# Block 0's MLP in seven half-size products per pair, with part of the weight splitting on GpSimd

## The reference

```
n = rmsnorm(x);  [pool in 512 | q 512 | k 128 | v 128 | pool gate 1024 | attn gate 1024] = n @ w_in
pool = (trailing means over 2/4/8/16 frames - frame) @ w_pool * pool_scale
attn = banded attention of q, k, v (8 query heads, 2 kv heads, rotary, sinks, window 2 chunks of 64)
h = x + (sigmoid(gp) * pool + sigmoid(ga) * (attn @ w_attn_up)) @ w_out
h = h + relu(rmsnorm(h) @ w_up)^2 @ w_down        # w_up 1024 x 4096, w_down 4096 x 1024
y = rmsnorm(h)
```

## Time and profile before

| | |
|---|---|
| median of 3 runs | 2354.0 us (2353.39 to 2355.53) |
| span of the profiled execution | 2351.3 us |
| instructions | 41109 |
| PE busy | 2325.9 us |
| DVE busy | 1642.2 us |
| ACT busy | 1075.6 us |
| GpSimd (POOL) busy | 350.2 us |

### The profile page before, as it was taken

The page is one execution under the profiler, slowest core; times in us unless marked ns, Lnnn a source line. Parts: engine busy times, 40 slices in busy tenths (PEclk is TensorE's granted clock), DMA queues, the critical chain, the costliest instruction groups (busy, mean ns, idle before and its releaser), DMA issues.

```text
span 2351.3 us, 41109 instructions
## 1 busy us (share of the span) xinstructions
PE 2325.9 (99%) x16389; PEld 2160.8 (92%) x16389; DVE 1642.2 (70%) x2462; ACT 1075.6 (46%) x1898; POOL 350.2 (15%) x272
## 2 busy tenths in 40 slices
PE   8999999999999999999999999999999999999997
PEld 8999999999987889999997788999998778999997
DVE  7645776465985568778687557876788656867766
ACT  4533434233435346456444435654463534645542
POOL 0500364563604000000003200000000400000000
PEclk9999999999999999999999999999999999999998
DMA  4223465565652237766753235767674223676674
GB/s 161 78 74 102 164 233 186 202 240 177 231 183 66 88 117 247 247 210 212 250 186 111 77 103 186 231 208 250 215 258 136 77 88 111 209 242 208 213 253 153
DMA packets 149166, 410.38 MB, mean 175 GB/s; under 512 B 17520, under 2 KB 17872, under 8 KB 144880
## 3 DMA queue, kind: packets, MB, share of 16 engines
q1 hardware_dynamic: 112128, 260.05, 33.9%
q10 hardware_dynamic: 36848, 147.70, 17.8%
HBM read 349.65 MB, written 58.13 MB: 173 GB/s over the span
## 4 chain that ended last, share of the span: by engine, by line
PE 98%; DVE 1%; DMA 1%; ACT 0%; issue 0%; DVEq 0%; SPq 0%; ACTq 0%
PE prod L509 53%; PE auxB L728 8%; PE auxB L729 8%; PE auxB L730 8%; PE prod L728 6%; PE prod L729 6%; PE prod L730 6%; PE auxB L509 1%; PE auxA L611 1%; PE auxB L641 1%; PE auxB L625 1%; PE auxA L509 0%; DMA wring<-weight_split 0%; DVE hT L1241 0%; DMA raw<-weights 0%; DVE wm L1189 0%
## 5 line engine op out<-in xcount | busy, mean ns | idle before, releaser
L509 PE MATMUL prod<-nH,wm 128*128 128x272 f32 (+1 forms) x3104 | 719.7, 333 | 8.2 <-DVE nL L1230 8.2
L509 PEld LDWEIGHTS prod<-nH,wm 128*128 128x128 f32 x3104 | 498.8, 189 | 67.9 <-DVE wm L1189 8.2
L772 ACT ACTIVATE wm<-raw 128x1024 fp32r<-128x1024 f32 x232 | 235.7, 1016 | 693.3 <-PE prod L509 685.2
L509 PE MATMUL prod<-nL,wm 128*128 128x272 f32 (+1 forms) x1552 | 438.8, 331 | 0.0
L772 ACT ACTIVATE wring<-rawq 128x512 fp32r<-128x512 f32 x492 | 303.3, 628 | 256.8 <-PE auxB L730 169.1
L1189 DVE TENSOR_TENSOR wring<-rawq,wring 128x512 fp32r<-128x512 f32 x492 | 334.8, 685 | 97.0 <-PE auxB L730 78.3
L1189 DVE TENSOR_TENSOR wm<-raw,wm 128x1024 fp32r<-128x1024 f32 x232 | 298.9, 1288 | 59.4 <-ACT wm L772 58.5
L509 PE MATMUL prod<-midH,wm 128*128 128x272 f32 (+1 forms) x1664 | 334.7, 313 | 0.2 <-DVE midL L1189 0.2
L509 PEld LDWEIGHTS prod<-nL,wm 128*128 128x128 f32 x1552 | 264.0, 189 | 26.7 <-issue 0.5
L509 PEld LDWEIGHTS prod<-midH,wm 128*128 128x128 f32 x1664 | 253.1, 188 | 18.2 <-issue 0.5
L728 PE MATMUL auxB<-m7H,wring 128*128 128x256 f32 x768 | 217.7, 283 | 0.8 <-DMA wring<-weight_split 0.6
(11 more groups left out here) (172 smaller groups left out, 4352.7 us busy)
## 6 DMA issues: line engine op xcount, KB each, us to landing
raw<-weights SPq DMA_DIRECT2D x200, 512.0 KB, 3.5
wring<-weight_split ACTq DMA_DIRECT2D x171, 512.0 KB, 4.8
rawq<-weights SPq DMA_DIRECT2D x288, 256.0 KB, 3.6
rawq<-weight_sums SPq DMA_DIRECT2D x204, 256.0 KB, 3.9
weight_split<-wsplit ACTq DMA_DIRECT2D x20, 1536.0 KB, 5.6
weight_sums<-wsum ACTq DMA_DIRECT2D x12, 1024.0 KB, 5.3
raw<-weights SPq DMA_DIRECT2D x32, 320.0 KB, 2.8
y<-hT ACTq DMA_DIRECT2D x12, 512.0 KB, 2.8
```

What stands on the lines that cost most here:

```text
L509: ins = nc.tensor.matmul(out[:, s, 0:hi - lo], lhs, rhs[:, lo:hi], start=first, stop=last)
L772: return nc.scalar.activation(out, in_, ACT.Copy, scale=scale)
```

## The change

Block 0's MLP now runs through `token` and `phase` as well, with halves of W0 = 272 columns. Its places in SBUF are its own (n0H/n0L, m0H/m0L, z0t, x_next), and its ring has 7 places. Its up phases after the first go in the order UP0 with `up_step0`, its down phases in DOWN0 with `down_step0`.

All its weights are split on the spot. The sums of phase 0 are made by GpSimd during block 0's mixer (`sum_early`) and go through DRAM; those of phases 1 to 7 stay in SBUF, one quarter a place (`slots`), and GpSimd makes them about two pairs ahead. SyncE's queue now loads the quarters, stores the sums, and stores each split quarter that blocks 1 to 3 will load straight from the ring (`after_split`); wsum and wsplit are gone. In phases 2, 4 and 6 GpSimd also makes the low part of tokens (0,4), (1,4) and (2,4). GpSimd adds up the squares of block 1's x at the end. Block 0's out products go in the order ORD.

```diff
+W0 = CMAX // 2
+UP0 = [(0, 1), (0, 5), (0, 2), (0, 6), (0, 3), (0, 7), (1, 1), (1, 5), (0, 4), (1, 6), (1, 3), (1, 2), (1, 7), (2, 1),
+       (2, 5), (1, 4), (2, 6), (2, 3), (2, 2), (2, 7), (3, 1), (3, 5), (3, 2), (3, 6), (3, 3), (3, 7), (2, 4), (3, 4)]
+DOWN0 = [(0, 1), (0, 5), (0, 2), (1, 1), (1, 5), (1, 2), (0, 6), (0, 3), (1, 6), (0, 7), (1, 3), (1, 7), (0, 4), (2, 5),
+         (1, 4), (2, 1), (2, 2), (3, 5), (2, 6), (2, 3), (3, 1), (3, 2), (2, 7), (3, 6), (2, 4), (3, 7), (3, 3), (3, 4)]
+RING0 = 7
...
+        by_pool = [("tok", 0, ph * NT7 + UP0.index((j, 4))) for ph in range(2, PHASES, 2) for j in range(3)]
...
+            def after_split(t):
...
+                wait_split_low(sp, "tok", 0, t)
+                if presplit(ph, r):
+                    slot, at = ring_slot(0, t), SPLIT_PHASES.index(ph) * PAIRS + j
+                    sp.dma_start(split_d[at, :, SUM[r], :, :], f(wring[:, slot, :, :])).then_inc(ring_out[slot], 16)
+                if ph == 0:
+                    return
+                if r == 5:
+                    store_sums(p)
+                if r == 1 and p + 2 <= LAST:
+                    wait(sp, s_S, p, 5)
+                    load_part(p + 2, "a11")
...
             for b in blocks:
                 for i in range(M_MLP):
                     mixer_product(b, i)
                     between(b, i)
-                if b == 0:
-                    for q in range(NQ):
-                        plain_up(q)
-                        plain_down(q)
-                else:
-                    for ph in range(PHASES):
-                        phase(b, ph)
+                for ph in range(PHASES):
+                    phase(b, ph)
...
+            def up_step0(q, k):
...
+                if k == 26:
+                    relu_z3(0, q, 2)
+                    sum_T13(0, q, 3)
+                    sum_T2(0, q, 3)
+                if k == 27:
+                    relu_z3(0, q, 3)
+                    low5(0, q, 3)
+                    sum_T4(0, q, 2)
+                weights_ahead(0, 2 * q * NT7 + k)
+                if k == 27:
+                    low2(0, q, 2)
+                    sum_T4(0, q, 3)
+                    low2(0, q, 3)
...
+            def sum_weights(p):
...
+                tt(a21, piece(p, "a11"), a21, ALU.subtract).then_inc(s_S.sem, 1)
...
+                tt(s6, a21, piece(p, "a22"), ALU.subtract).then_inc(s_S.sem, 1)
...
+                tt(piece(p, "s5"), s6, piece(p, "a11"), ALU.subtract).then_inc(s_S.sem, 1)
...
+                tt(piece(p, "s3"), piece(p, "a12"), s6, ALU.add).then_inc(s_S.sem, 1)
+
+            def low_by_pool(ph, j):
+
+                t = ph * NT7 + UP0.index((j, 4))
+                slot = wring[:, ring_slot(0, t)]
+                pool.wait_ge(w_high, split_no["tok", 0, t])
+                tt(slot[:, 1, :], piece(PAIRS * ph + j, "a22"), f(slot[:, 0, :]), ALU.subtract).then_inc(pool_low, 1)
```

More of the change, by code:

```diff
@@ L82, with order @@
 SPLIT_PHASES = (0, 2, 4, 6, 7)
-HALF = (0, 0, 1, 0)
-SHIFT = (0, 4, 0, 4)
+HALF = (0, 1, 0, 1)
+SHIFT = (4, 0, 4, 0)
+FK0 = [0, 1, 4, 5, 2, 6, 3, 7]
 FK = [0, 1, 4, 5, 2, 3, 6, 7]
+def order(b, ph):
+    return ORDER if b > 0 or ph == 0 else DOWN0 if ph % 2 else UP0
 def presplit(ph, pr):
@@ L253, in build @@
         s_r = Signal("root_inverted", norms)
-        plain = [("x", 0), ("h", 0)] + [("x", b) for b in later]
+        plain = [("x", b) for b in blocks]
         s_nH = Signal("gained_high", [(*n, k) for n in plain for k in range(KD)])
@@ L313, in build @@
         s_H5, s_L5, s_H2, s_L2 = (Signal(f"hid7_{n}", ups) for n in ("high5", "low5", "high2", "low2"))
-        s_add = Signal("down_product_added", [(b, q, j, r) for b in later for q in range(NQ) for j, r in ORDER if r != 2])
+        s_add = Signal("down_product_added", [(b, q, j, r) for b in blocks for q in range(NQ) for j, r in order(b, 1) if r != 2])
         def wait(eng, signal, *item):
@@ L478, in _ @@
+            for b in later:
+                if b == 1:
+                    wait_token(sp, 0, TOKENS - 1)
+                    for s in range(2):
+                        sp.wait_ge(sums_out[s], sums_count[LAST - 1 + s])
+                    for s in range(RING):
+                        if ring_stored[s]:
+                            sp.wait_ge(ring_out[s], ring_stored[s])
                     sp.dma_start(xT[:, :, 0:TB], x123[0, :, :, :]).then_inc(x_in, 16)
-            for b in later:
-                for i in range(RAW if b > 1 else 0, M_MLP):
+                for i in range(RAW, M_MLP):
@@ L908, in step @@
                         gain_pair_high(b, m)
-                        for t in raw_tokens(b, 5, RING):
+                        for t in raw_tokens(b, 5, ahead(b)):
                             split_high_token(b, t)
@@ L1600, in add_product, with down_step0 @@
                 else:
-                    tt(h, h, bank_c(j) if r == 5 else bank_a(j), ALU.add).then_inc(s_add.sem, 1)
+                    tt(h, h, bank_c(b, j) if r == 5 else bank_a(b, j), ALU.add).then_inc(s_add.sem, 1)
+            def down_step0(q, k):
+                j, r = DOWN0[k]
+                if r != 2:
+                    add_product(0, q, j, r)
+                weights_ahead(0, (2 * q + 1) * NT7 + k)
+                if q < NQ - 1:
+                    return
+                if k % 2 and 7 <= k < 7 + 2 * KD:
+                    gained_low(1, (k - 7) // 2)
+                if k in (21, 22, 23, 24):
+                    invert_part("x", 1, k - 21)
+                if k == 26:
+                    scale_angles(1)
+                if k in (25, 26):
+                    split_low(1, k - 25)
+                for n, at in ((1, 18), (2, 19), (3, 20), (4, 21), (5, 26), (6, 27), (7, 27)):
+                    if k == at:
+                        add_square("f", 0, n)
```

760 lines of the change are left out of this document (428 added, 332 removed).

## The result

The changed kernel takes **2406.1 us** in the median (2403.7 to 2408.3, four runs), and the kernel before, on the same chip, 2353.8: a ratio of 1.0223 with a 95% interval of 1.0208 to 1.0237. It is 52 us slower, where 24 us of gain were forecast, and it lies outside the range of 2308 to 2354.

What follows compares the result with a forecast made beforehand. PE, busy 99%, was taken as the bound: 48.3 us saved, less 20.5 of standing in up phases and 4 on the way into block 1, made 23.8 gained, 2354.0 to 2330 us. Eight in ten: 2308 to 2354.

Steps and rivals of the forecast that it cites:

- Term 1: Block 0's MLP products on PE: 2688 matmuls instead of 3072, at 0.1257 us each, saving 48.3 us.
- Terms 2 and 3: Block 0's up phases: DVE's 38.9 us plus 13.3 lost beside GpSimd; PE stands 5.5 us in phases 2, 4, 6.
- the named sign: Profile after, block 0's up phases: wring lows near 1.2 us in the mean where GpSimd runs.
- The law "1.1 us times DVE's share of two-SBUF work": Block 0's MLP: what one GpSimd instruction costs DVE, put at 0.7 us in an up phase.
- rival B: Block 0's up phases: DVE becomes the bound outright, losing 1.1 us per GpSimd instruction; 2366 us, chance 0.08.
- Term 3's phase 0: Block 0's first up phase: DVE needs 52.0 us with about 9 GpSimd instructions, so PE stands 4 us.
- Term 4: Block 0's down phases: DVE needs 34.3 us against 34.7 left, so it just fits; 0 us.
- Term 5: Last down phase, into block 1: some 17 us of extra DVE work; PE stands 4 us, between 0 and 10.
- DMA stands at a share of 0.59: Transfers in block 0's MLP stretch: about the same bytes after the change, counted among what costs nothing.
- A: Block 0's MLP: PE stays the bound and stands 0 to 12 us; centre 2310 us, chance 0.27.
- C: Block 0's MLP: GpSimd itself is late, 35 instructions per two phases taking 91 us; 2344 us, chance 0.1.
- D: Block 0's up phases: the lows on GpSimd bring nothing; price 0, inside the forecast, no chance of its own.

Runs made afterwards that it cites:

- experiment 1: Changed kernel with GpSimd's additions and nine low parts replaced by constant writes that read nothing: 2356.65 us, ratio 1.0014 to the kernel before.
- Experiments 3 and 4: Changed kernel: first, the nine low parts back on DVE, 2394.95 us; second, those lows on GpSimd but its additions replaced by constants, 2356.3 us.
- experiment 7: Changed kernel with the squares of block 1's input taken up six tokens later in phase 7: 2402.55 us, ratio 1.0205.
- experiment 9: Changed kernel with block 1's squares six tokens later and GpSimd writing constants in place of its additions and low parts: 2352.0 us, ratio 0.9993.

## Why the prediction was wrong, by its own steps

**Term 1 was right.** 48.3 us were to be saved by 2688 matmuls at 0.1257 us; they run at 0.1259, and where nothing disturbs an up phase (experiment 1) it takes 43.36 us for 336 of them.

**Terms 2 and 3, the up phases, failed in size and in the place of the wait**, though the mechanism (GpSimd's reads hold DVE up, and PE waits for DVE) was the right one and the named sign (wring lows near 1.2 us) is there, at 0.98 and 1.18. The sum let PE wait only where the next phase needs its last operand, m0L. It never waits there. It waits inside the phases, 28.4 us for line 1529 and 21.3 us for hT to read PSUM banks and 16.0 us for low parts. They said 53.7 us of need against 48.2, so 5.5 us of standing. Taken over two phases, as the window that reaches 7.5 us into the next phase demands, up and down together were to last 84.4 + 5.5 = 89.9 us; phases 2 and 3 last 103.9. The 14 us are in three pieces:

- DVE's own work: 38.9 + 26.9 = 65.8 forecast, 35.2 + 33.3 = 68.5 in experiment 1. 2.7 us. (An up phase's tail falls into the next down phase, so only the sum of the two compares.)
- The loss beside GpSimd: 13.3 + 7.4 = 20.7 forecast. Measured as the difference in DVE's busy time between the changed kernel and experiment 1: 50.7 - 35.2 = 15.5 and 44.5 - 33.3 = 11.2, 26.7 us, 0.81 and 0.74 us for each of the 19 and 15 GpSimd instructions, where 0.7 and 0.46 had been worked out. 6.0 us. The law "1.1 us times DVE's share of two-SBUF work" came out low by 15% in up phases and by more in down phases, and the traces count why. In the kernel before, 65 of the 120 GpSimd instructions held a DVE one up (it is longer than the shortest of its form), by 0.9 us in the mean, 58 us in all or 0.48 each; the forecast's 46 us and 0.39 took in three groups only. In the changed kernel 117 of 128 do, again by 0.85 us in the mean. The price of a hit is nearly the same, and the share of hits went from 54% to 91%: a DVE that is late has the next such instruction ready, the very thing that rival B said. The Trainium skill ("SBUF — State Buffer", section "Who interferes with whom") has it that the two exclude each other for a whole instruction, and that a GpSimd instruction that only writes leaves DVE alone. The trace agrees with both: the lows end 0.55 us after the GpSimd instruction that they begin under, and in experiment 1 they are at 696 ns beside 29 us of writes. The prediction took the rule to mean a price of 1.3 us and not 1.1; the rows give 1.1 under the same rule. The low of 390.48 begins 0.11 us behind GpSimd's 1.34 us and runs 0.55 us beyond its end, 0.14 less than its own 0.69: 1.34 - 0.11 - 0.14 = 1.1.
- DVE waiting itself: 3.4 us in all forecast (1.5 before token 0, 1.5 for ACT in the tail, and 0.4 to spare in the down phase); measured 103.9 - 95.1 = 8.8 us. 5.4 us. DVE serves its queue in order, so a wait for ACT or for PE in the middle of a phase isn't made up for by room elsewhere.

The error behind them is that a phase was weighed as one window, in which 48.2 us of room meet 53.7 us of need. The room is not one: in the 12.5 us before (1,4) DVE loses 6.5 us, because GpSimd's eight instructions between tokens 8 and 15 run back to back. Experiments 3 and 4 point the same way: with the additions reading, nine lows on GpSimd cost 11 us; with the additions only writing, their reads cost nothing.

**Term 3's phase 0** was put at 4 us: phase 0 is 13.7 us over its bare 42.3, and 9.4 over it even in experiment 1. **Term 4** said 0 us for down phases; 4.8 and 5.2 us in phases 3 and 5, and 11.2 in phase 1, whose start still waits for the tail of phase 0's order (a gap of 4.4 to 4.9 us at (1,2), with GpSimd's reads and without).

**Term 5, the way into block 1**, is the one that was mis-sized most: 4 us (0 to 10) were taken, and phase 7 is 22.4 us over the bare phase, 25.3 in experiment 1. The sum counted DVE instructions (17 us of them). What it put at nothing is that ACT takes the input's squares in its queue ahead of copies of quarters: it waits for the transfer of x_next and then for GpSimd's part of the squares, 16 us with two steps, and quarters' copies stand behind. Moving these waits took away 5 us of the phase (experiment 7) and 7 (experiment 9), so they are a part of the 22 and not the whole. From ACT's timeline of the changed kernel:

```profile
660.93 0.63 ACT L916 ACTIVATE sq<-x_next 128x512 f32<-128x512 f32 x1 [8.64 <-DMA x_next<-x]
...
671.16 0.63 ACT L916 ACTIVATE sq<-x_next 128x512 f32<-128x512 f32 x1 [7.43 <-POOL work L1836]
```

The first of them falls in a stretch in which every DMA engine is taken. "DMA stands at a share of 0.59" was a mean over 385 us.

The whole: 24.5 us of standing were forecast, 100.5 are there. Of the 76 more, about 29 are the contention (49.5 by experiment 1, 20.5 forecast) and 47 what stands without it: the entry and the exit of the MLP, where experiment 1 has 41 us in phases 0, 1 and 7, and 8 us in the phases between. Either alone would have put the time outside the forecast's range. Without GpSimd's reads the kernel ties with the one before, so **the 50 us of contention and the 50 us that stand without it use up the 48 us saved, each by itself**.

**The rivals.** A (PE stays the bound) is excluded by 78 us of gaps. So is C (GpSimd late) for the up phases: in experiment 1 GpSimd is as busy (29 us of 43), and PE hardly stands in phases 2, 4 and 6. B, at 0.08, is what happened in sign and in kind, though its 2366 is 40 us short: its price for the point of change was 1.06 us per GpSimd instruction, and 0.81 sufficed since the ends cost nearly 40 us more than it knew. D said that the lows on GpSimd bring nothing; they cost 11 us. The clock was in no step. It showed, and cost about 5 us.

**Open:** what the remaining 16 us of phase 7 hang on once GpSimd's reads are gone and the transfers are apart, and the 9 and 6.5 us of phases 0 and 1 without those reads (in phase 7 DVE is busy for 46.9 of 67.6 us in experiment 1, so it isn't its work alone); and whether an order of DVE's queue exists in which its doing the additions pays.

## What to carry to other kernels

Where an engine's queue is in order and tight, don't weigh its time per phase: take the dozen microseconds before the instruction that PE waits for next, be it an operand or the read that frees a PSUM bank, and add up what stands in the queue there, each instruction at its disturbed length. Price work given to a second engine by what it does to the first when both are always ready, not by the present mean, which has idle time in it. And count the entry and the exit of a changed stage from its own queue orders and transfers: here they cost as much as the stage saved.

## What the runs showed of the hardware that was not expected

- A GpSimd instruction that reads SBUF and a DVE instruction with two SBUF inputs take turns, and each waits for the rest of the other: in the changed kernel's phases 1 to 6, 72 lengthened lows end 0.55 us after the GpSimd instruction that they begin under, and an addition of 1.29 us by itself takes up to 2.68 beside DVE.
- GpSimd's writes alone leave DVE free: 363 of them in the MLP, 192 us busy, lows at 696 ns; additions of full width give 982 and 1177 ns, of half width 791 and 833.
- The granted clock was 0.54 in the 5.5 us after PE had stood for 4.9, and the matmuls there were spaced 0.22 instead of 0.126 us, near the 1.2 GHz level. Keeping PE at work with matmuls that nobody reads held the clock at 1.00 in phase 2 (0.98 over the MLP, for 0.94), and gave only 5 us, since most of the loss had lain in time for which PE would have waited anyway.
- With the DMA engines' share at 0.99 to 1.02 (342 to 413 GB/s) loads of 256 KB landed 8.5 and 8.9 us after their issue, against a median of 3.4.
